# Triangular inverses of a delta-rule recurrence: quarter products, transposes in place of a third product, a projection cut into pieces

## The reference, cut to what matters

```python
def rwkv7_bidir_branch(p, mu, w0, w2, a0, a2, k_k, k_a, r_k, lnx_g, lnx_b):
    shifted = jnp.stack([shift_prev(pf), shift_next(pf)])
    q = pf[None] + mu[:, None, None, :] * (shifted - pf[None])
    r, k, v, wd, ad = jnp.split(q, RWKV_SPLITS, axis=-1)
    ...
    _, y = lax.scan(wkv7_step, init, xs)        # 512 tokens, each direction

def wkv7_step(state, inp):
    r, w, k, v, a, b = inp
    sa = jnp.einsum('...ij,...j->...i', state, a)
    state = (state * w[..., None, :] + sa[..., :, None] * b[..., None, :]
             + v[..., :, None] * k[..., None, :])
    y = jnp.einsum('...ij,...j->...i', state, r)
    return state, y
```

## Time and profile before

| | |
|---|---|
| median of 3 runs | 4398.61 us (4394.69 to 4404.72) |
| profiled execution | 4397.82 us, its span 4396.0 us |
| the 16 steps of `wkv` | from about 3511 to 4290 us of the span |
| PE, DVE, ACT, POOL busy | 96%, 57%, 36%, 8% of the span |
| granted clock of PE, mean | 0.983 |

### The profile page before, as it was taken

The page is one execution under the profiler, slowest core; times in us unless marked ns, Lnnn a source line. Parts: engine busy times, 40 slices in busy tenths (PEclk is TensorE's granted clock), DMA queues, the critical chain, the costliest instruction groups (busy, mean ns, idle before and its releaser), DMA issues. The chain is left out here.

```text
span 4396.0 us, 77246 instructions
## 1 busy us (share of the span) xinstructions
PE 4212.1 (96%) x32340; PEld 3167.3 (72%) x32340; DVE 2490.7 (57%) x4058; ACT 1590.7 (36%) x2471; POOL 341.4 (8%) x313
## 2 busy tenths in 40 slices
PE   8898999999999999999999999989999999999988
PEld 6675788786688867888887644467887567766775
DVE  3635534433544351778778499964544256665663
ACT  2325322323422241666666310143233133334332
POOL 0030000000000000111111000000000022222220
PEclk9898999999999999999999999999999999999999
DMA  4301222222122232212211322222223100000101
GB/s 157 116 21 68 86 96 96 102 94 87 58 96 96 110 135 99 68 56 61 65 55 46 153 77 77 77 77 77 96 106 135 72 24 22 22 22 21 47 16 58
DMA packets 37637, 334.95 MB, mean 76 GB/s; under 512 B 4192, under 2 KB 6496, under 8 KB 19680
## 3 DMA queue, kind: packets, MB, share of 16 engines
q1 hardware_dynamic: 37344, 330.66, 20.5%
HBM read 318.06 MB, written 12.58 MB: 75 GB/s over the span
## 5 line engine op out<-in xcount | busy, mean ns | idle before, releaser
L654 PE MATMUL ps<-hi,weight_parts 128*128 128x512 f32 x3072 | 957.4, 392 | 26.7 <-DVE lo L430 17.9
L642 DVE TENSOR_TENSOR weight_parts<-w,weight_parts 128x1024 fp32r<-128x1024 f32 (+1 forms) x327 | 398.0, 1219 | 906.2 <-ACT weight_parts L633 905.6
L633 ACT ACTIVATE weight_parts<-w 128x1024 fp32r<-128x1024 f32 (+1 forms) x327 | 343.9, 1053 | 999.4 <-PE ps L654 906.1
L654 PEld LDWEIGHTS ps<-hi,weight_parts 128*128 128x128 f32 x3072 | 580.1, 189 | 156.5 <-issue 23.5
L654 PE MATMUL ps<-lo,weight_parts 128*128 128x512 f32 x1536 | 600.4, 391 | 0.0
L4297 PEld LDWEIGHTS ps<-buffers 64*64 64x64 f32 x12544 | 413.0, 135 | 127.3 <-issue 126.7
L654 PE MATMUL ps<-hidden_high,weight_parts 128*128 128x512 f32 x1536 | 491.7, 399 | 12.5 <-DVE hidden_low L428 12.5
L4297 PE MATMUL ps<-buffers 64*64 64x64 f32 x12544 | 438.4, 224 | 42.7 <-issue 21.1
L2821 PE MATMUL ps<-x_parts,column_parts 128*128 128x512 f32 x1536 | 359.8, 392 | 5.0 <-DVE column_parts L3081 4.4
L654 PEld LDWEIGHTS ps<-hidden_high,weight_parts 128*128 128x128 f32 x1536 | 290.3, 189 | 80.1 <-issue 17.3
L654 PEld LDWEIGHTS ps<-lo,weight_parts 128*128 128x128 f32 x1536 | 290.4, 189 | 60.2 <-issue 0.2
(11 more groups left out here) (584 smaller groups left out, 5903.9 us busy)
## 6 DMA issues: line engine op xcount, KB each, us to landing
w<-in_weights SPq DMA_DIRECT2D x121, 2048.0 KB, 8.7
w<-in_wh SPq DMA_DIRECT2D x64, 512.0 KB, 3.9
buffers<-in_weights SPq DMA_DIRECT2D x3, 2048.0 KB, 12.8
x_kept<-x SPq DMA_DIRECT2D x2, 2048.0 KB, 7.8
v_kept<-buffers SPq DMA_DIRECT2D x4, 1024.0 KB, 5.3
buffers<-v_kept SPq DMA_DIRECT2D x16, 256.0 KB, 2.6
x<-in_xT SPq DMA_DIRECT2D x4, 512.0 KB, 11.3
h<-in_pw SPq DMA_DIRECT2D x2, 1024.0 KB, 5.6
```

The lines of the kernel that those rows point to most:

```text
L633: act.activation(K.parts[:, j % 2, 0, 0:nk, :], part_of(K, slot, j, nk, by_row), ACT.Copy)\
L642: dve.tensor_tensor(K.parts[:, j % 2, 1, 0:nk, :], part_of(K, slot, j, nk, by_row), K.parts[:, j % 2, 0, 0:nk, :].bitcast(F32), ALU.subtra ...
L654: mm = pe.matmul(ps, K.parts[:, j % 2, m, k, :], x[:, k * T:(k + 1) * T], start=(first and k == 0 and n == 0), stop=(last and k == nk - 1 ...
```

## The change

- X is no longer updated by a product of its own. Instead XT is transposed before each level: four 128x128 transposes (two chunks each) into a bank of PSUM (`xr0` to `xr4`), copied by VectorE to X. This gives X with the chunk's parity, not the head, as the half of the partitions.
- So t takes its result in that layout, and t and ct are products on four quarters of the array: upper and lower rows combined with left and right columns, in the order (0,0), (1,1), (0,1), (1,0). The two halves of rows write different banks.
- t is copied by ScalarE (bank 0) and VectorE (bank 1). Each level has one t and one ct group; the split into halves a and b is gone, and so is cx. VectorE's addition to XT is one of 512 columns.
- `projection(1)` is cut into eight products (`piece`), one or two to a level.
- The next step's mixing moves from the head into levels 1 to 4 (GpSimd's products in 1 to 3, VectorE's in 2 to 4), and its squares of k to level 4 on ScalarE; `kkn` stands right after `wa`. Step 0 still does its own in its head.
- ScalarE's `keep` calls stand after the exponentials and at the step's end; the second part of `finish` stands after the exponentials on ScalarE and after the third copy of G on VectorE.

```diff
@@ gpsimd: behind C of levels 1 to 3 @@
+                    if l < 4:
+                        mixed(after(n), l - 1)
@@ tensor @@
+            quarters = ((0, 0), (1, 1), (0, 1), (1, 0))
+                def piece(k):
+                    if nth is None:
+                        return
+                    if k == 0:
+                        pe.wait_ge(K.sem("raw_kept"), K.count("raw_kept", 4 * (c + 1) + 2 * d))
+                        pe.wait_ge(DM.sem, DM.count(n, "mrk"))
+                    q, m = 1 - par, 2 * d + 1
+                    w = K.W[:, (first + q) % 2, :].rearrange("p (k n) -> p k n", k=8)
+                    mm = pe.matmul(K.ps[:, 3, :], w[:, k, m * P:(m + 1) * P], K.H[:, k, :], start=(k == 0), stop=(k == 7),
+                                   skip_group_check=True)
...
                 for l in levels:
                     if n is not None:
+                        if l == 1:
+                            pe.wait_ge(AM.sem, AM.count(n, "as"))
+                        pe.wait_ge(DM.sem, DM.count(n, f"xt{l - 1}"))
+                        for u in range(4):
+                            mm = pe.transpose(K.ps[:, 1 if l == 1 else 2, u * P:(u + 1) * P],
+                                              XT[:, 2 * u:2 * u + 2, :].rearrange("p e t -> p (e t)"), K.c("ident"))
+                        mm.then_inc(PM.step(f"xr{l - 1}"), 1)
                         pe.wait_ge(GM.sem, GM.count(n, f"c{l}"))
-                        for half in "ab":
-                            pe.wait_ge(DM.sem, DM.count(n, f"xt{l - 1}{half}" if l > 1 else "x0"))
-                            for j in chunks_of(half):
-                                mm = heads(block_of(0, j), C[:, j, :], XT[:, j, :])
-                            mm.then_inc(PM.step(f"t{l}{half}"), 1)
+                        if l == 1:
+                            pe.wait_ge(DM.sem, DM.count(n, "x0"))
+                        for u in range(4):
+                            for h, e in quarters:
+                                mm = pe.matmul(two_banks(0)[hr(e), u, h, :], paired(C)[hr(h), u, e, :],
+                                               paired(XT)[hr(h), u, e, :], start=True, stop=True, skip_group_check=True)
+                        mm.then_inc(PM.step(f"t{l}"), 1)
                     ch_g(p, pd, l + 2)
+                    if n is not None and 1 < l < 5:
+                        piece(2 * l - 3)
                     if n is not None:
+                        pe.wait_ge(AM.sem, AM.count(n, f"t{l}"))
+                        pe.wait_ge(DT.sem, DT.count(n, f"t{l}"))
+                        pe.wait_ge(DM.sem, DM.count(n, f"x{l - 1}" if l > 1 else "mrb"))
...
+                                mm = pe.matmul(two_banks(4)[hr(h), u, e, :], paired(X)[hr(e), u, h, :],
+                                               paired(T1)[hr(e), u, h, :], start=True, stop=True, skip_group_check=True)
                     ch_sa(p, pd, l + 2)
-                    if n is not None and l < 5:
...
-                                mm = heads(block_of(2, j), T1[:, j, :], X[:, j, :])
+                    if n is not None:
+                        piece(2 * l - 2 if l < 5 else 7)
                     ch_ys(p, pd, l + 2)
@@ scalar @@
+                        act.activation(paired(T1)[:, :, 0, :], two_banks(0)[:, :, 0, :], ACT.Copy).then_inc(AM.step(f"t{l}"), 1)
                     san(p, pd, l + 2)
+                    if l == 4:
+                        squared(after(n))
+                if nth is not None:
+                    if d == 1:
+                        act.wait_ge(K.sem("fin_dve"), K.count("fin_dve", 4 * c))
+                    keep(c + 1, 1 - par, 2 * d + 1)
@@ vector, levels @@
+                    if n is not None and l > 1:
+                        dve.wait_ge(PM.sem, PM.count(n, f"xr{l - 1}"))
+                        dve.tensor_copy(X.rearrange("p j t -> p (j t)"), K.ps[:, 2, :]).then_inc(DM.step(f"x{l - 1}"), 1)
+                    if n is not None:
+                        dve.wait_ge(PM.sem, PM.count(n, f"t{l}"))
+                        dve.tensor_copy(paired(T1)[:, :, 1, :], two_banks(0)[:, :, 1, :]).then_inc(DT.step(f"t{l}"), 1)
                     gk(p, pd, l + 2)
+                    if 1 < l < 5:
+                        mixed(after(n), l - 2)
                     if n is not None:
+                        dve.tensor_tensor(paired(XT if l < 5 else XTC[:, d]), paired(XT), two_banks(4), ALU.add)\
+                           .then_inc(DM.step(f"xt{l}"), 1)
                     upd(p, pd, l + 2)
```

More of the change, by code:

```diff
@@ L4263, in step @@
                 pool.tensor_copy(W2F, W2[:, ds(d * 1024 + c * P, P)]).then_inc(GM.step("w2f"), 1)
[L4264 to L4268, removed]
+                if n == 0:
+                    for m in range(3):
+                        mixed(n, m)
                 pool.wait_ge(DM.sem, DM.count(n, "khat"))
                 K.apart(pool)
-                pool.tensor_copy(X, on_chunks("cident")).then_inc(GM.step("ix"), 1)
                 pool.tensor_copy(XT, on_chunks("cident")).then_inc(GM.step("ixt"), 1)
@@ L4366, in step @@
                                      stop=True).then_inc(PM.step("wa"), 1)
+                    pe.wait_ge(SQ.sem, SQ.count(n, "sqk"))
+                    pe.wait_ge(DM.sem, DM.count(n - 1, "xt5"))
+                    pe.matmul(K.ps[:, 4, :], same, K.sq[:, 0, :], start=True, stop=True).then_inc(PM.step("kkn"), 1)
                 ch_g(p, pd, 0)
                 if fin is not None:
-                    pe.wait_ge(DM.sem, DM.count(n - 1, "xt5b"))
+                    pe.wait_ge(DM.sem, DM.count(n - 1, "xt5"))
                     finish(0, *fin)
@@ L4373, in step @@
                 ch_sa(p, pd, 0)
[L4374 to L4377, removed]
                 if fin is not None:
@@ L4444, in step @@
                     if n is not None:
[L4445 to L4452, removed]
-                                mm = heads(block_of(4, j), X[:, j, :], T1[:, j, :])
-                            mm.then_inc(PM.step(f"ct{l}{half}"), 1)
@@ L4455, in step @@
-                    ch_sa(p, pd, l + 2)
-                    if n is not None and l < 5:
-                        if l == 1:
-                            pe.wait_ge(DM.sem, DM.count(n, "mrk"))
-                            K.apart(pe)
-                        for half in "ab":
-                            for j in chunks_of(half):
-                                mm = heads(block_of(2, j), T1[:, j, :], X[:, j, :])
-                            mm.then_inc(PM.step(f"cx{l}{half}"), 1)
+                        pe.wait_ge(AM.sem, AM.count(n, f"t{l}"))
@@ new lines, in step @@
+                        pe.wait_ge(DT.sem, DT.count(n, f"t{l}"))
+                        pe.wait_ge(DM.sem, DM.count(n, f"x{l - 1}" if l > 1 else "mrb"))
+                        K.apart(pe)
+                        for u in range(4):
+                            for e, h in quarters:
+                                mm = pe.matmul(two_banks(4)[hr(h), u, e, :], paired(X)[hr(e), u, h, :],
+                                               paired(T1)[hr(e), u, h, :], start=True, stop=True, skip_group_check=True)
@@ L4678, in step @@
                 gk(p, pd, 2)
+                if fin is not None:
+                    finish(1, *fin)
                 if n is not None:
                     strict, incl = ("clt", "cle") if d == 0 else ("cgt", "cge")
[L4681 removed]
+                    up = "cup0" if d == 0 else "clow0"
                     dve.wait_ge(GM.sem, GM.count(n, "ixt"))
@@ L4719, in _ @@
             rounds(dve, step, finish)
-    for m in (PM, AM, DM, GM):
+    for m in (PM, AM, DM, GM, MX, MP, SQ, DT):
         m.done(16)
```

134 lines of the change are left out of this document (73 added, 61 removed).

## The result

The changed kernel takes 4423.23 us (median of 5 runs, 4421.14 to 4426.31), the kernel before 4398.61. The ratio is 1.0056, 95% interval 1.0045 to 1.0067: slower by 24.6 us, where +51 was forecast. The profiled execution has a span of 4422.8 us.

A forecast was written before the change was run, and what follows sets the result against it. TensorE, busy 96% of the span, was taken to bound the kernel. Head -1.8, levels +3.7 and clock +2.0 made +3.9 us a step, +51 over 13 steps: 4449 us, range 4388 to 4510.

The forecast's parts named there:

- point 5: Head with one projection: 28.6 us to the recurrence's chunk 3 in direction 0, 29.5 in direction 1; mean -1.8 us.
- The waits before `tb` and `bon`: In the new head: TensorE idle about 2 us before tb and 1 us before the sum at L4400.
- Transposes: Four full-array transposes a level in place of the cx products: 0.74 us a run, +3.05 us in the levels.
- a piece: One eighth of the second projection, in the levels: 1.06 us, 1.18 with change-over; eight add +9.4 us.
- a full level: One level holds 5.1 us of TensorE work against a dependency chain of 4.8, so TensorE still decides.
- The four quarters: t and ct products in the levels: 14.7 ns an instruction instead of 29.3, 4.2 us less.
- point 6: Levels summed: 21.4 us plus 0.9 of waits, 22.3 against 18.65, so +3.7 us a step.
- point 7: Loosely filled heads make the granted clock fall in most steps: 0 to 3.4 us a step, taken as 2.0.
- A: Rival: four quarters as forecast but the clock holds, +25 us, 4423 us; chance 0.13.
- B: Rival: quarters gain nothing, TensorE accepts no more than one small instruction in 29 ns, 4504 us; chance 0.22.
- The case of 25 ns: Starts never closer than about 25 ns: t and ct groups save 1.2 us, not 4.2; 4488 us; chance 0.07.
- C: Rival: head not held by the chain through ScalarE, all 7.2 us leave it, -1.4 us a step, 4380 us; chance 0.12.

The follow-up runs named there:

- e1_fill: Changed kernel plus products nobody reads in TensorE's waits (ahead of bhat, rk and x0), steps 0 to 13: 4406.95 us, 1.0030 of the kernel before.
- e3_split0: Changed kernel with the first projection split: products 0 to 4 stay, 5 to 7 go into the waits for bhat and rk: 4384.57 us, 0.9980 of before.
- e11_one_quarter: Changed kernel with t and ct products ordered quarter by quarter, so neighbours use the same quarter: 4517.57 us, 1.0271 of the kernel before.
- e8_before_wide: Kernel before with the eight small cx products of a half done as two of 256 columns (other sums in X): 4394.45 us, ratio 0.9995.
- e5_level1: Changed kernel with VectorE's state update ahead of two masked products at level 1, and piece(0) behind ys(3): 4406.31 us, 1.0021 of the kernel before.
- e7_both: Changed kernel with both the split first projection and the new order at level 1: 4366.45 us, 0.9932 of the kernel before.
- e10_small: e7_both with the first seven pieces of the second projection replaced by 18 small products each with constants: 4380.32 us, 0.9958 of the kernel before.

## Why the prediction was wrong in size

The direction was right, and the mechanisms named were found, though not all at the size given; the time was +24.6 us where +51 stood. A steady step was to get 3.9 us longer and got 2.1.

| term, us a step | predicted | measured | from |
|---|---|---|---|
| head | -1.8 | -1.9 | 31.05 to 29.14 (e1_fill) |
| levels | +3.7 | +2.7 | 18.98 to 21.69 (e1_fill) |
| clock | +2.0 | +1.3 | 52.13 less 50.83 (e1_fill) |
| 13 steps (us in all) | +51 | +27.3 | |
| the rest, in the profiled executions (us in all) | 0 | -0.5 | spans, +26.8 |
| median against these executions (us in all) | 0 | -2.2 | +24.6 |

**The head (point 5) held.** 28.6 and 29.5 us were forecast, 28.74 (e1_fill, direction 0) and 29.61 came out. In step 4 of the changed kernel (direction 0) ScalarE's table load starts 10.18 us after the step's start and VectorE's first product 12.80, where 10.2 and 12.8 were forecast. The waits before `tb` and `bon` are where they were put, though shorter: 1.8 and 1.2 us (directions 0 and 1) and 0.7 where 2.0 and 1.0 stood. The copy of X and the update stand in the way as forecast, and e3_split0 bears out the chain behind ScalarE's copy. The term compared with the before of two steps, 30.06 and 31.55; over 13 steps that was 31.05, since pauses fell into some heads.

**Single prices held.** Transposes 0.74 us a run (0.58 to the next start and 0.16 ahead), a piece 1.06 us and its change of form, a full level 5.00 (5.1). The four quarters' 15.5 ns lie near the 14.7 forecast, but that is luck: 14.7 was a quarter of 58.6, a single quarter's spacing read off the pairs of `heads`, and a single quarter has 40.7 (e11_one_quarter). A quarter of that would be 10.2, so what sets the 15.5 is open.

**The step that failed is the sum of the levels (point 6), with the clock (point 7).** Two things made the levels' difference too large by 1.0 us a step, 13 us in all. First, the 0.9 us of waits added for the copies of t were 0.3: 21.4 was nearly all (measured 21.67). Second, the number subtracted. The 18.67 us came from one step; the mean of 13 is 18.98, and it can be as low as 17.33 (step 12). The prediction called the 1.8 us over TensorE's own 16.9 "waits" and did not ask what ended them. Over the 13 steps 13.2 us, 1.0 a step, were pauses without a releaser in the levels; in the changed kernel's full level there is no wait left. A third of the way from 51 to 24.6 lies in the clock: the price was bounded by one fall of 6.8 us a step at half speed; they are 3.4 us each, 14 in 13 steps, and e1_fill prices all at 1.3 us a step, 0.7 less than taken (9 us). The head adds 1 us. The last 2.7 us are the two bottom rows of the table, of which the 0.5 is inside the error given for the other steps.

**The rivals.** A (the clock holds, 4423) gave the right time by luck: the clock fell in 9 of 13 steps and cost 17 us, and what a steady clock would have saved was saved for the most part in the levels. B (quarters gain nothing) fell with the 15.5 ns. The case of 25 ns fell too. The Trainium skill's page TensorE: Matmul & The Clock Gate (section "Wait — 56ns, not 53.3ns?") says that starts come no closer than about 25 ns; the traces have 23.2 ns on two quarters and 15.5 on four, so for products that take turns on quarters the measurement decides against it. C (the head not bound by the chain) fell: the head was bound just so.

## What to carry to other kernels

Take the time before from many steps and ask what ends each gap: a gap without a releaser that returns after a fixed count of instructions is not a wait of the program, and a change that thins the stream can take it away (the changed kernel did, e8_before_wide did not). Here work taken off the engine that bounds left holes, and the holes cost the clock: products of the same stage put into them (e3_split0) gave 3.1 us a step, and even useless ones (e1_fill) gave 1.3. In an engine's own queue, an update on which another engine waits goes ahead of work that is wanted later (e5_level1).

## What the runs showed of the hardware that I had not expected

- The instructions of 64x64 products start 15.5 ns apart when four quarters take turns, 23.2 ns on two quarters with two banks, 29.3 on two with one bank, 40.7 on one.
- TensorE paused 0.2 to 2.1 us, 123 to 126 matmul instructions apart or a multiple of that within a step, where small ones came dense: 13.8 us between 3400 and 4150 us in the kernel before, none in e7_both's steps 1 to 13, back in e10_small. Each of 71 pauses ended 2.2 to 3.0 us after a packet of the instruction queue had started.
- The granted clock fell in pieces of 3.4 us in the changed kernel (three of 6.8 in e5_level1), in steps whose full levels had no gap; the waits, of 0.2 to 1.8 us, lay in the head and before chunk 3.
